# Layer norm of the convolution mixer: the output products ordered anew around its steps

## The reference, cut to what matters

```python
def conv_module(val, gate, w_dw, b_dw, ln_g, ln_b, w_pw, b_pw):
    h = val * jax.nn.sigmoid(gate)
    h = lax.conv_general_dilated(h, w_dw[:, None, :], ...) + b_dw   # 31 taps, 384 channels
    h = jax.nn.silu(layer_norm(h, ln_g, ln_b))
    return h @ w_pw + b_pw

        ya = pool_mixer(a, pool_w[l], pool_scale[l])        # 256 channels
        yb = gmlp_mixer(u, v, gm_norm_g[l], gm_ws[l], gm_b[l])   # 384
        yc = conv_module(cv, cg, ...)                        # 384
        x = x + jnp.concatenate([ya, yb, yc], axis=-1) @ w_out[l]
```

## Time and profile before

| what | us |
|---|---|
| median of 3 runs | 1889.71 |
| lowest and highest | 1885.68, 1889.85 |
| the profiled execution, its own time | 1888.1 |
| its span, first to last instruction | 1886.3 |
| PE busy | 1834.0 (97%) |
| DVE busy | 1487.1 (79%) |
| ACT busy | 1166.1 (62%) |

### The profile page before, as it was taken

The page is one execution under the profiler, slowest core; times in us unless marked ns, Lnnn a source line. Parts: engine busy times, 40 slices in busy tenths (PEclk is TensorE's granted clock), DMA queues, the critical chain, the costliest instruction groups (busy, mean ns, idle before and its releaser), DMA issues.

```text
span 1886.3 us, 25920 instructions
## 1 busy us (share of the span) xinstructions
PE 1834.0 (97%) x10249; PEld 1594.3 (85%) x10249; DVE 1487.1 (79%) x1633; ACT 1166.1 (62%) x1103; POOL 56.2 (3%) x71
## 2 busy tenths in 40 slices
PE   7999999999999999998999999999999999999997
PEld 7888988899888999996888888888888888888886
DVE  6664667766796655696889889988898898998897
ACT  4445656555553533544777777777777777777775
POOL 0000000000320000220000000000000000000000
PEclk9999999999999999999999999999999999999999
DMA  9434433755462756464899999999999999999993
GB/s 324 140 106 134 158 112 112 231 197 183 140 196 68 232 187 201 136 196 150 291 379 368 354 349 370 361 374 360 344 361 367 366 374 344 363 367 367 381 357 114
DMA packets 258047, 495.70 MB, mean 263 GB/s; under 512 B 9625, under 2 KB 99455, under 8 KB 257919
## 3 DMA queue, kind: packets, MB, share of 16 engines
q1 hardware_dynamic: 253263, 489.04, 73.8%
q10 hardware_dynamic: 4656, 4.93, 0.9%
HBM read 492.89 MB, written 1.05 MB: 262 GB/s over the span
## 4 chain that ended last, share of the span: by engine, by line
PE 88%; DVE 6%; ACT 4%; issue 1%; DMA 0%; DVEq 0%; SPq 0%; ACTq 0%
PE bank L438 27%; PE bank L440 27%; PE bank L439 27%; DVE splitL L398 3%; ACT splitH L394 2%; PE bank L2192 1%; PE bank L2123 1%; PE bank L1798 1%; DVE co L1670 1%; PE bank L1906 1%; PE bank L1200 0%; PE bank L2161 0%; PE bank L2162 0%; PE bank L899 0%; ACT RAH L480 0%
## 5 line engine op out<-in xcount | busy, mean ns | idle before, releaser
L398 DVE TENSOR_TENSOR splitL<-raw,splitH 128x2048 fp32r<-128x2048 f32 (+1 forms) x338 | 768.9, 2278 | 177.3 <-ACT splitH L394 169.3
L394 ACT ACTIVATE splitH<-raw 128x2048 fp32r<-128x2048 f32 (+1 forms) x338 | 641.3, 1902 | 151.7 <-PE bank L440 132.9
L438 PE MATMUL bank<-splitH,RBH 128*128 128x512 f32 x960 | 380.1, 396 | 1.5 <-DVE rr L2058 0.9
L440 PE MATMUL bank<-splitH,RBL 128*128 128x512 f32 x960 | 374.4, 390 | 0.0
L439 PE MATMUL bank<-splitL,RBH 128*128 128x512 f32 x960 | 374.1, 390 | 0.0
L438 PE MATMUL bank<-RAH,splitH 128*128 128x256 f32 x1088 | 311.5, 286 | 7.9 <-DVE RAL L484 3.8
L439 PE MATMUL bank<-RAL,splitH 128*128 128x256 f32 x1088 | 307.7, 283 | 0.0
L440 PE MATMUL bank<-RAH,splitL 128*128 128x256 f32 x1088 | 307.7, 283 | 0.0
L438 PEld LDWEIGHTS bank<-RAH,splitH 128*128 128x128 f32 x1088 | 208.3, 191 | 12.2 <-ACT RAH L480 6.8
L440 PEld LDWEIGHTS bank<-splitH,RBL 128*128 128x128 f32 x960 | 180.2, 188 | 38.6
L438 PEld LDWEIGHTS bank<-splitH,RBH 128*128 128x128 f32 x960 | 180.4, 188 | 38.1 <-issue 1.8
(11 more groups left out here) (324 smaller groups left out, 2246.8 us busy)
## 6 DMA issues: line engine op xcount, KB each, us to landing
raw<-in_moe_wg SPq DMA_DIRECT2D x71, 1024.0 KB, 5.9
raw<-in_moe_wu SPq DMA_DIRECT2D x71, 1024.0 KB, 6.2
raw<-in_moe_wd SPq DMA_DIRECT2D x69, 1024.0 KB, 6.1
rawx<-in_moe_wd SPq DMA_DIRECT2D x29, 1024.0 KB, 5.9
rawx<-in_moe_wu SPq DMA_DIRECT2D x28, 1024.0 KB, 6.1
rawx<-in_moe_wg SPq DMA_DIRECT2D x27, 1024.0 KB, 5.8
raw<-in_w_in SPq DMA_DIRECT2D x24, 1024.0 KB, 6.5
raw<-in_w_up SPq DMA_DIRECT2D x22, 1024.0 KB, 5.1
```

The costliest lines, as they stand in the source:

```text
L394: a = act.op(lambda e: e.activation(h[:, 0:size], r[:, 0:size], ACT.Copy), self.landed[n], over)
L398: d = dve.op(lambda e: e.tensor_tensor(l[:, 0:size], r[:, 0:size], h[:, 0:size].bitcast(F), ALU.subtract), self.landed[n], over, a)
L438: e.matmul(o, lh, rh, start=start, stop=False)
L440: return e.matmul(o, ll, rh, start=False, stop=stop)
```

## The change

Slab 1's first chunk is done in two halves of 6 matmuls, for positions 0 to 127 ahead of the column sum and for 128 to 255 behind it. Slab 1's second chunk moves from behind the column sum to behind the variance products. Slab 2's first chunk moves from behind the variance products to behind the spread. Slab 4's split is begun in the same place, but its residual on VectorE moves from ahead of centring to behind it. Slab 5's split begins on ScalarE behind slab 1's second chunk, thus after the variance products in the order of the code, and no longer ahead of them. The diff:

```diff
@@ -1846,19 +1846,24 @@
             Wt = W.take("mo", 0)
             down(Wt, catH, catL, [(0, 0), (1, 1)], True, False, by=cat)
             W.release(Wt[3], pe.now())
-            W.ahead(3)
-            Wt = W.take("mo", 0)
-            down(Wt, catH, catL, [(0, 2)], False, False, by=cat)
+            rest_of_split = W.begin_split()
+            Wt = W.take("mo", -1)
+
+            def down_half(tb, kcs):
+                for i in (2 * tb, 2 * tb + 1):
+                    tstat(Wt, banks[i][:, :], catH, catL, tb, kcs, (512 * (i % 2), 512 * (i % 2) + 512), False, False,
+                          by=cat)
+
+            down_half(0, [(0, 2)])
             b, t = colsum(co, list(tc.values()))
-            down(Wt, catH, catL, [(1, 3)], False, False, by=cat)
-            W.release(Wt[3], pe.now())
+            down_half(1, [(0, 2)])
             td = []
             for u in range(3):
                 t1 = dve.op(lambda e, u=u, b=b: e.scalar_tensor_tensor(
                     dd[:, u, :], banks[b][:, 0:256], -INV, co[:, u, :], ALU.mult, ALU.add), t)
                 td.append(act.op(lambda e, u=u: e.activation(sq[:, u, :], dd[:, u, :], ACT.Square), t1))
             ps.free[b] = [t1]
-            rest_of_split = W.begin_split()
+            rest_of_split()
             b = ps.take()
 
             def f(e, b=b):
@@ -1868,10 +1873,9 @@
                                         ones[:, 0:2], start=(u == 0), stop=(u == 2))
                 return last
             t = pe.op(f, td, ps.free[b])
-            Wt = W.take("mo", 0)
-            down(Wt, catH, catL, [(0, 4)], False, False, by=cat)
-
-
+            down(Wt, catH, catL, [(1, 3)], False, False, by=cat)
+            W.release(Wt[3], pe.now())
+            rest_of_split = W.begin_split()
             t = [dve.op(lambda e, b=b, tb=tb: e.tensor_scalar(
                 stat(5, 8, tb), banks[b][:, 2 * tb:2 * tb + 1], -0.5 * INV, -0.5 * EPS, ALU.mult, ALU.add), t)
                 for tb in range(2)]
@@ -1888,6 +1892,8 @@
                 return last
             t = pe.op(f, t, ps.free[b])
             rstd = banks[b][:, 0:256]
+            Wt = W.take("mo", -1)
+            down(Wt, catH, catL, [(0, 4)], False, False, by=cat)
             ts = []
             for u in range(3):
                 t1 = dve.op(lambda e, u=u: e.tensor_tensor(dd[:, u, :], dd[:, u, :], rstd, ALU.mult), t)
```

## The result

| what | us |
|---|---|
| before, 12 executions: median (lowest to highest) | 1885.87 (1884.33 to 1890.04) |
| after, 12 executions: median (lowest to highest) | 1882.86 (1881.20 to 1883.94) |
| ratio of after to before | 0.9978, 95% interval 0.9971 to 0.9985 |
| the profiled execution: before, after | 1888.1, 1881.2 |
| its span: before, after | 1886.3, 1879.4 |

The kernel became faster by 0.22%, and the interval leaves no change out. The medians differ by 3.0 us, the means (1886.64 and 1882.70) by 3.9. I had forecast a gain of 3.5 us, but also that it would most likely count as no change.

What follows compares the result with a forecast made beforehand. TensorE was taken to bound the kernel (88% of the chain), so gains lie in its idle or low-clock time. Queues 2 x 0.90 plus clock 1.70 gave 3.5 us off 1888.9: 1885.4 us, range 1882.4 to 1889.2.

Steps and rivals of the forecast that it cites:

- column sum issued: TensorE's column sum, now after 6 slab 1 products, would wait 0.05 us for the taps (bounds 0 and 0.15).
- variance products issued: TensorE would wait for the squares before the variance products, a new idle piece of 0.65 us.
- spread issued: After the root on VectorE, the spread would issue 2.02 us earlier, at 579.27 against 581.29.
- silus start: ScalarE's silus, queued behind slab 5's split, would start 1.1 us late, at 581.71 rather than 580.60.
- The gain of the queues: Pointwise products in each of two mixer calls would start 0.90 us earlier, stretch 12.95 from 13.85; bounds 0.7 and 1.58.
- The split in ScalarE's queue: Slab 5's split, first in first out ahead of the silus, limits each call's gain to 0.90 us; otherwise 1.58.
- The later DMAs: Weight DMA issued by SP after slab 4's residual would come 1.7 us later, at no cost to TensorE.
- The clock: Low clock in call 1's pointwise products would go, 5.47 to 3.77 us: 1.70 gained, bounds 0 and 3.40.
- The level: Starting time for the whole kernel: 1888.9 us, the middle of four executions, from which 3.5 was subtracted.
- 0.76 for no change: Chance that the whole time stays within about 0.3% (5.7 us); faster had 0.22, slower 0.02.
- Slower, by the clock: Rival, 5%: two new idle pieces per call bring TensorE to 1.2 GHz in both calls; +3.3 us, 1892.2.
- More than the sum: Rival, 17%: silus not held up, or timed runs had the clock's fall in both calls; 1884.0, 1883.7 or 1882.3.

Runs made afterwards that it cites:

- e1: Changed kernel with slab 5's split moved, its ScalarE half behind the three silus, its VectorE half behind the last pointwise evacuation; 1881.74 us, repeated 1881.51.
- e3: Changed kernel with slab 4's residual ahead of centring again, the regrouped products kept; median 1889.77 us against 1885.88 for the kernel before.
- e4: Changed kernel with both row halves of slab 1's first chunk ahead of the column sum; median 1888.33 us against 1885.88 for the kernel before.
- e6: Kernel before with only slab 2's first chunk moved behind the spread; median 1890.59 us against 1885.88.
- e5: Kernel before with only slab 4's residual moved behind centring; median 1885.99 us against 1885.88, ratio 0.9995.
- e8: e4 plus 8 extra products, their result unread, in the wait before the variance products; median 1885.68 us against 1885.88 for the kernel before.

## Why the prediction was right or wrong

*The steps.* Taken from the start of slab 1 (570.40 in the prediction, 568.70 in the profile), they compare so:

| step | forecast | after |
|---|---|---|
| column sum issued | 1.43 | 1.36 |
| centring starts | 3.16 | 3.08 |
| variance products issued | 4.75 | 4.67 |
| root starts | 6.45 | 6.28 |
| spread issued | 8.87 | 8.64 |
| slab 5's split starts on ScalarE | 9.35 | 9.12 |
| silus start | 11.31 | 10.94 |
| pointwise products issued | 12.95 | 12.56 |

Every step came in the order and for the reason given. (One sentence of the prediction says that 12 products move from ahead of the column sum to behind the variance products; they stood behind the column sum, as its own timeline has it, and the sum is not touched by the slip.) The column sum in call 0 did not wait for the taps; in call 1 it issued at 853.13, 1.41 after slab 1's start at 851.72, thus 0.05 late. The variance products take 1.33 us rather than 1.45 when TensorE comes to them from a wait, and the silus start 0.1 before the split's recorded end. **The gain of the queues was mis-sized: 1.28 us for each call, where I had 0.90** (bounds 0.7 and 1.58). Of the 0.39 by which the pointwise products come earlier than forecast in the table, 0.23 are there at the spread, and 0.14 more come in at the silus, which start 1.82 after the split rather than 1.96.

*The split in ScalarE's queue.* Right, and shown by e1. The silus are ready from 578.64 and start at 579.64, behind a split that itself waited for TensorE until 577.82. The rule that ScalarE takes its instructions in order (the Trainium skill, TensorE: Matmul & The Clock Gate, the section on the array's architecture) agrees with that. The measured gain of 1.28 lies between the 0.90 with the rule and the 1.58 without it, so the gain alone would not have decided; the rows of ScalarE do, and e1, which gains 13.85 - 11.81 = 2.04 up to the pointwise products once the split is out of the way.

*The later DMAs.* No wait of TensorE for a weight DMA appeared, and the gain of call 0 was handed on whole to call 1 (the first pointwise product of call 0 is 2.99 us earlier, the start of slab 1 in call 1 2.98).

*The clock.* I put 1.70 us into the sum as if each execution had the fall. In the profiled execution it went, as forecast; over many it is worth the difference between the gain of the means, 3.95, and the queues' 2.56, thus 1.4 us, and 0.4 in the medians. The whole record bears the queues' part out: without its upper cluster the kernel before has a median of 1885.10, the changed kernel's 22 have 1882.67, and that is 2.4 less, beside the 2.56 of the stretches. Two terms were off in opposite directions, and the sum of 3.5 lies between the gain of the medians (3.0) and of the means (3.9). That is luck in part.

*The level.* 1885.4 was counted from 1888.9, the middle of four executions, three of which belong to the upper cluster (1889.85, 1889.71 and the profiled 1888.1). The median of 12 is 1885.87. From there the same sum gives 1882.4; measured were 1882.86, near the lower end of my range.

*The chances.* **The step that failed is the last: 0.76 for no change.** By the sum and all rivals but two (12% together) the kernel is faster by 1.8 to 6.6 us. I set that aside because 0.3%, or 5.7 us, was taken for what a measurement of this kernel can tell, a term for which the prediction gives no row and which no run bears out. What the runs showed in its place: twelve executions of each kernel give an interval of 0.14% in width, and the gain of 0.22% (3.0 us) stands clear of it. A gain of 3.5 us that is carried by a chain of timed steps should have stood as a forecast of faster, small but real.

*The rivals.* "Slower, by the clock" named the right mechanism and the wrong kernel: it happened in e3, e4 and e6, where one idle piece of 2.0 to 2.4 us borders on the variance products, and in neither profile of the change, where the pieces are 0.68 and 0.78. "More than the sum" did not come.

## What to carry to other kernels

When work is regrouped around a chain over several engines, lay out all queues together. The residual's place was worth nothing alone and 1.6 us a call in company, and the chunk behind the spread was a loss alone. Look at what else the move sets in front of a step: the split that moved with its release took back 0.75 us a call up to the pointwise products, and 0.6 on the whole. And where idle time can bring the clock down, one profile and three executions give a wrong level; count how many executions show it before putting it into a sum.

## What the runs showed that I had not expected

Two idle pieces of nearly the same length brought the lower clock at very different rates, by the place in which they lay. With 2.32 us ahead of the pointwise products the mean clock was 0.993 or less in 20 of 92 executions (the kernel before and e5). With 2.41 us next to the variance products (12 matmuls of 2 columns), and the same work otherwise, it was in all 10 of e6, and both calls of its profile show 1.2 GHz. With 2.31 and 2.03 us there it was in 7 of 11 of e3 (one call of its profile) and in 10 of 11 of e4 (both calls), though these two have a second idle piece of 0.4 to 0.8 us further on. That the place counts is shown by e6 against the kernel before; why it counts no run shows. Such a fall cost 16.73 - 13.91 = 2.8 and 17.12 - 13.93 = 3.2 us in e4's profile, counted against the filled e8; eight useless products of 1.8 us in the wait made that kernel faster.
